# Conditioning panels accumulated on DVE, another order of the first chunks, and a tile-by-tile pass from the last layer norm to the first RMS norm

## The reference

```python
s_c = silu(c); s_cc = silu(c_ctx)
for i in range(DEPTH):                                   # DEPTH = 2
    m  = (s_c  @ ada_w[i] + ada_b[i]).reshape(B, 9, 1, D)
    mc = (s_cc @ ada_w[i] + ada_b[i]).reshape(9, D)      # the context's
    x = half_step_ffn(x, m[:, 0], m[:, 1], m[:, 2], ...)
    ...
# half_step_ffn: y = (silu(a) * u) @ w_out with a, u = split(modulate(x) @ w_in)
#                x = layer_norm(DN_ALPHA * x + 0.5 * gate * y, g, b)
```

## Time and profile before

| | us |
|---|---|
| median of 3 runs | 3017.51 |
| lowest and highest | 3009.21 and 3021.42 |
| profiled execution | 3014.72 |
| its span | 3012.9 |
| TensorE busy (96% of the span) | 2898.0 |
| DVE busy (59%) | 1765.8 |
| ACT busy (45%) | 1356.7 |

### The profile page before, as it was taken

How to read it: one execution, slowest core, us unless ns; L and a number is a source line. 1 busy time by engine, 2 the same in 40 slices (tenths; PEclk the granted TensorE clock), 3 DMA queues, 4 the chain that set the end, 5 groups by cost and what they waited for, 6 DMA issues and landing times. The chain is left out here.

```text
span 3012.9 us, 51229 instructions
## 1 busy us (share of the span) xinstructions
PE 2898.0 (96%) x19396; PEld 2540.7 (84%) x19396; DVE 1765.8 (59%) x2644; ACT 1356.7 (45%) x1928; POOL 375.3 (12%) x306
## 2 busy tenths in 40 slices
PE   6999999899999999999899999999999999999998
PEld 3667765677888889888899989899999998988998
DVE  2323224267766667666545866757855577566784
ACT  1222213125655544554344544455644454436563
POOL 2111100113110110211100120201101002020110
PEclk8999999999999999999999999999999999999999
DMA  9986354751565655465435505245555451533564
GB/s 325 285 252 195 103 164 130 198 168 49 158 184 154 194 183 160 148 195 182 142 120 167 161 28 176 92 134 153 170 162 161 137 154 57 160 114 112 161 179 135
DMA packets 586157, 474.79 MB, mean 158 GB/s; under 512 B 28721, under 2 KB 547889, under 8 KB 585665
## 3 DMA queue, kind: packets, MB, share of 16 engines
q1 hardware_dynamic: 584464, 460.44, 49.8%
q0 software_dynamic: 1520, 11.95, 1.3%
HBM read 471.23 MB, written 4.72 MB: 158 GB/s over the span
## 5 line engine op out<-in xcount | busy, mean ns | idle before, releaser
L2309 DVE TENSOR_TENSOR low<-raw,high 128x1024 fp32r<-128x1024 f32 (+1 forms) x744 | 904.6, 1219 | 801.0 <-ACT high L2079 798.6
L2079 ACT CAST high<-raw 128x1024 fp32r<-128x1024 f32 (+1 forms) x744 | 768.1, 1034 | 987.9 <-PE PS L1987 604.7
L1985 PE MATMUL PS<-NHh,high 128*128 128x272 f32 (+1 forms) x2304 | 669.0, 290 | 11.4 <-DVE NHl L1752 6.9
L1987 PE MATMUL PS<-NHh,low 128*128 128x272 f32 (+1 forms) x2304 | 660.8, 287 | 0.0
L1986 PE MATMUL PS<-NHl,high 128*128 128x272 f32 (+1 forms) x2304 | 660.0, 286 | 0.0
L1985 PEld LDWEIGHTS PS<-NHh,high 128*128 128x128 f32 x2304 | 433.3, 188 | 16.9 <-issue 9.1
L1986 PEld LDWEIGHTS PS<-NHl,high 128*128 128x128 f32 x2304 | 433.9, 188 | 0.8
L1987 PEld LDWEIGHTS PS<-NHh,low 128*128 128x128 f32 x2304 | 433.6, 188 | 0.0
L1983 PE MATMUL PS<-XX,high 128*128 128x512 f32 x966 | 347.8, 399 | 0.0
L1985 PE MATMUL PS<-XX,high 128*128 128x512 f32 (+1 forms) x752 | 273.5, 364 | 6.9 <-DVE XX L2370 4.4
L1982 PE MATMUL PS<-XX,low 128*128 128x256 f32 x966 | 272.4, 282 | 1.4 <-DVE XX L2370 1.0
(11 more groups left out here) (351 smaller groups left out, 4868.7 us busy)
## 6 DMA issues: line engine op xcount, KB each, us to landing
raw<-w_in_dram SPq DMA_DIRECT2D x416, 256.0 KB, 3.0
raw<-ffn_w_in_dram SPq DMA_DIRECT2D x352, 256.0 KB, 3.4
part<-ada_w_dram SPq DMA_DIRECT2D x184, 256.0 KB, 4.2
raw<-w_ffn_in_dram SPq DMA_DIRECT2D x176, 256.0 KB, 3.2
raw<-ffn_w_out_dram SPq DMA_DIRECT2D x160, 256.0 KB, 3.1
raw<-w_branch_dram SPq DMA_DIRECT2D x96, 256.0 KB, 3.0
raw<-w_ffn_out_dram SPq DMA_DIRECT2D x80, 256.0 KB, 3.0
part_sg<-ada_w_dram SPq DMA_DIRECT2D x48, 256.0 KB, 3.0
```

Of the source, the lines that this page charges most:

```text
L1985: nc.tensor.matmul(out, wh, xh, start=begin, stop=False)
L1987: last = nc.tensor.matmul(out, wl, xh, start=False, stop=end)
L2079: nc.scalar.copy(high[:, slot, 0:nk, :], raw[:, slot, 0:nk, :]).then_inc(s_high, 1)
L2309: nc.vector.tensor_tensor(low[:, slot, 0:nk, :], raw[:, slot, 0:nk, :], high[:, slot, 0:nk, :].bitcast(F32), ALU.subtract).then_inc(s_low, 1)
```

## The change

Three edits are made together.

1. **Conditioning.** Parts of panels 4 to 35 are no longer multiplied on TensorE. `ada_accumulate` on DVE multiplies a row tile of the part by the column `silu` and adds it to an accumulator of 128x512: two operations for a part, and four for the first six panels (`ADA_BOTH` = 10), whose context half is needed too. It is called in `split_low(S)` for the parts hosted at S-4. TensorE sums four accumulators over the partitions with a column of ones (`ada_sum`, two chunks behind the turn's last host). Hosts, buffers and dues are new; SP's `load_part` now waits for `s_adak`, which DVE raises.
2. **Start.** The first chunks of units 0 and 1 come first, with panel 3's parts between them, then the second chunks of both; the low tiles of X are made two at a time; `keep_warm` issues idle matmuls; chunk 1's weights are loaded before panel 1.
3. **Norms.** DVE scales each tile by `xg` and rdev, ACT squares it with the bias `xb`, and DVE writes `H` beside that. The second constants have a semaphore of their own.

```diff
-ADA_HOSTS = ((0, 32, 80), (44, 24, 24), (68, 16, 24))
+ADA_HOSTS = ((2, 12, 16), (14, 10, 16), (24, 10, 16), (34, 6, 8), (45, 38, 72))
+ADA_BOTH = 10
@@ def turn_host(t)
-    return HOST[4 * TURN * t - 1]
+    return min(HOST[4 * TURN * t - 1] + 2, 83)
@@ buffers
+        ROWS, TAIL, TOP = range(4, 11), 11, (12, 13)
+        part_slot = [A % 4 if HOST[A] < 32 else A % 2 if HOST[A] < 44 else
+                     ROWS[A % 7] if HOST[A] < 68 else 11 + A % 3 for A in range(ADA_PARTS)]
+        def place(s, u, c):
+            return 2 * c + u if s is steps[0] and isinstance(u, int) and u < 2 else s["S0"] + len(s["kch"]) * u + c
@@ issue
-            due = HOST[before] + 4 if before is not None else {PSG: 47, PRS: 47, TAIL: 71}.get(part_slot[A], 1)
+            due = HOST[before] + 4 if before is not None else 3 + part_slot[A] if HOST[A] < 44 else 48 if HOST[A] < 68 else 71
@@ def load_part(A)
                 if before is not None:
-                    sp.wait_ge(s_ada, 4 * ADA_FIRST + before + 1)
+                    sp.wait_ge(s_adak, before + 1)
+                elif slot in ROWS:
+                    sp.wait_ge(s_chunk, steps[1]["S0"] + 4)
+                elif slot in TOP:
+                    sp.wait_ge(s_res, KT + 4)
@@ TensorE
+            def ada_sum(t):
+                pe.wait_ge(s_adak, 4 * TURN * t)
+                pe.wait_ge(s_adarow, max(1, t - 1))
+                for c in range(2):
+                    for x in range(TURN):
+                        both = TURN * t + x < ADA_BOTH
+                        if both or not c:
+                            last = nc.tensor.matmul(PS[32 * x:32 * x + 32, ROW_BANK + t % 2, :],
+                                                    ONEW[:, 2 * (TURN - x) - 1 - c:2 * (TURN - x) + 31 - c], ada_acc(t, x, c),
+                                                    start=not c, stop=bool(c) or not both)
+                last.then_inc(s_adasum, 1)
...
-                        for A in ada_parts(S + c):
-                            ada_part(ADA_FIRST + A // 4, A % 4)
+                        if isinstance(at, int) and at in sum_after:
+                            ada_sum(sum_after[at])
...
+                    if s is steps[0]:
+                        for c in range(2):
+                            for u in range(2):
+                                gemm_unit(u, u, 0, 0, c)
+                                if c == 0 and u == 0:
+                                    for q in range(4):
+                                        ada_part(3, q)
@@ DVE, def split_low(S, slot, nk)
+                for A in ada_parts(S - NSLOT if isinstance(S, int) else S):
+                    ada_accumulate(A)
+
+            def ada_accumulate(A):
+                n, c = ADA_FIRST + A // 4, A % 4
+                t, x = divmod(n, TURN)
+                slot = part_slot[A]
+                dve.wait_ge(s_part[slot], 32 * part_slot[:A + 1].count(slot))
+                if x == 0 and c == 0 and t > 1:
+                    dve.wait_ge(s_adasum, t - 1)
+                for y in range(2):
+                    k = 2 * c + y
+                    src = flat(parts_at[slot][:, 2 * y:2 * y + 2, :])
+                    for e in range(2 if n < ADA_BOTH else 1):
+                        acc, factor = ada_acc(t, x, e), silu[:, KT * e + k:KT * e + k + 1]
+                        if k == 0:
+                            ins = nc.vector.tensor_scalar(acc, src, factor, None, ALU.mult)
+                        else:
+                            ins = nc.vector.scalar_tensor_tensor(acc, src, factor, acc, ALU.mult, ALU.add)
+                        if y == 0 or e < (n < ADA_BOTH):
+                            link(ins)
+                ins.then_inc(s_adak, 1)
+                dve.wait_ge(s_adak, A + 1)
@@ ACT, last layer norm
-                        act.wait_ge(s_res, 6 * KT + KT)
-                        act.wait_ge(s_meta, 32)
-                        for v in range(4):
-                            rms_act_pair(act, 0, v, None)
+                        act.wait_ge(s_meta, 16)
+                        nc.scalar.activation(TQ[:, :, 0:N_META], H[:, :, 0:N_META], ACT.Square)
+                        for k in range(KT):
+                            act.wait_ge(s_modd, KT * 6 + k + 1)
+                            ins = nc.scalar.activation(TQ[:, k, N_META:T2], TC[:, k, 0:T], ACT.Square,
+                                                       bias=sm("xb")[:, k:k + 1])
+                            if k % 2:
+                                ins.then_inc(s_rsq, 1)
+                        act.wait_ge(s_con2, 16)
@@ DVE, last layer norm
-                        standardise(0)
-                        standardise(1).then_inc(s_modd, 1)
+                        for k in range(KT):
+                            nc.vector.scalar_tensor_tensor(TC[:, k, 0:T], TC[:, k, 0:T], sm("xg")[:, k:k + 1],
+                                                           RS[:, 1, 0:T], ALU.mult, ALU.mult).then_inc(s_modd, 1)
+                        for k in range(KT):
+                            dve.wait_ge(s_modd, KT * 6 + k + 1)
+                            nc.vector.tensor_scalar(H[:, k, N_META:T2], TC[:, k, 0:T], sm("xb")[:, k:k + 1], None,
+                                                    ALU.add).then_inc(s_res, 1)
```

More of the change, by code:

```diff
@@ L317, in two_block_kernel @@
         SC0 = 2 * (TURN - 1)
-        SCW = E1.take("SCW", [P, KT, SC0 + 32])
         adarow = E1.take("adarow", [P, T1])[:]
+        acc2 = E1.take("acc2", [P, PW])
+        scw_at = E1.at
+        acc3 = E1.take("acc3", [P, PW])
+        SCW = Region(scw_at).take("SCW", [P, KT, SC0 + 32])
+        ONEW = E1.take("ONEW", [P, 2 * TURN + 31])
+        silu = E1.take("silu", [P, 2 * KT])
         e1_end = E1.at
@@ L494, in behind, with finished @@
                     two(i)
+        def place(s, u, c):
+            return 2 * c + u if s is steps[0] and isinstance(u, int) and u < 2 else s["S0"] + len(s["kch"]) * u + c
+        def finished(s, u):
+            return s["S0"] + len(s["kch"]) * (u + 1) + 4 + (s is steps[0] and isinstance(u, int) and u == 0)
         def unit_of(S):
@@ L514, in issued_after @@
             return [A for A in range(ADA_PARTS) if issue[A] == S] if isinstance(S, int) else ()
+        sum_after = {turn_host(t): t for t in range(1, ADA // TURN)}
         turn_unit = [None] + [unit_of(turn_host(t)) for t in range(1, ADA // TURN)]
@@ L1716, in rms_squares @@
         def rms_squares(m):
-            return SQ if m and m % 2 == 0 else TN
+            return TN if m % 2 else SQ if m else TQ
         def rms_pe_pair(pe, m, v):
@@ L1800, in load_unit @@
                         sp.wait_ge(s_low, S + 1)
-                    if not isinstance(S, int) or S:
+                    if isinstance(S, int) and S < NSLOT:
+                        if S > 1:
+                            load(raw[:, S], s_raw[S], s["src"](S - 2, *SHALLOW[1]))
+                    else:
                         load(raw[:, slot], s_raw[slot], s["src"](u, k0, nk))
@@ L1807, in _ @@
                 if n == 1:
-                    load(raw[:, 0], s_raw[0], steps[0]["src"](0, *SHALLOW[0]))
+                    for u in range(2):
+                        load(raw[:, u], s_raw[u], steps[0]["src"](u, *SHALLOW[0]))
                 for c in range(4):
@@ L1873, in ada_fold, with keep_warm @@
                 return last
+            def keep_warm(n):
+                for _ in range(n):
+                    nc.tensor.matmul(PS[0:32, 4, :], SCW[:, 0, 0:32],
+                                     raw0[:, 4 * FIRST_PLACE[0], 0:2, :].rearrange("p a n -> p (a n)"),
+                                     start=True, stop=True)
             pe.wait_ge(s_sc4, 3)
-            for n in (0, 2, 1, 3):
+            for n in (0, 2, 1):
+                if n == 2:
+                    keep_warm(9)
                 if n == 1:
@@ L1950, in rows_ready, with gemm_unit @@
                         pe.wait_ge(s_hl, s["hid0"] + 2 * c)
-                def gemm_unit(u, p, S, slot0):
+                def gemm_unit(u, p, S, slot0, only=None):
                     kch = s["kch"]
                     for c, (k0, nk) in enumerate(kch):
-                        pe.wait_ge(s_low, S + c + 5)
+                        if only is not None and c != only:
+                            continue
+                        at = S + c if only is None else place(s, u, c)
+                        pe.wait_ge(s_low, at + 5)
                         rows_ready(u, c, k0 + nk)
@@ L1960, in gemm_unit @@
                                 pe.wait_ge(s_oln, half_first(s["layer"], 2) + 1)
-                        slot = (slot0 + c) % NSLOT
+                        slot = (slot0 + c) % NSLOT if only is None else at
                         for j in range(2):
-                            if isinstance(S, int) and S + c == 0 and j == 1:
+                            if isinstance(at, int) and at == 1 and j == 1:
                                 ada_columns(0)
@@ L2099, in residual_rows @@
```

(10 more changed lines are left out.)

79 lines of the change are left out of this document (41 added, 38 removed).

## The result

| | before | after |
|---|---|---|
| median | 3018.39 us | 3333.64 us |
| lowest and highest | 3009.21 and 3021.42 | 3330.33 and 3335.39 |
| profiled execution's span | 3012.9 | 3333.6 |

The changed kernel is slower by 10.5%: the ratio is 1.105, with a 95% interval of 1.1026 to 1.1074. The prediction was 3290 us, from 3215 to 3350, so the sign and the range held, and the forecast was 44 us short.

What follows compares the result with a forecast made beforehand. TensorE, 96% busy, bounds the kernel before; after the change SP's in-order load queue, tied to DVE's accumulations, does. 3014.7 us + 283 (later milestones up to q) - 8 (norm) = 3290 us, range 3215 to 3350.

Steps and rivals of the forecast that it cites:

- The bound and the sign: SP's load queue, waiting for DVE's accumulations, lets one chunk be in flight at a time; slower, chance 0.93.
- TensorE was to idle for `low`: First third of the changed profile: TensorE idles before L2035, released by `low`, and its busy share falls to some 85%.
- The untied rival: SP's load queue: the tie doesn't bind because parts or raws run further ahead; 2902 us, chance 0.05.
- The cycle: From one accumulated chunk to the next: 8.2 us plus the accumulation, 9.7 to 14.0 us, where TensorE needs 5.5.
- The operation: One DVE accumulation on 128x512: 0.72 us, bounds 0.63 and 0.80; 219 us in all.
- longer-cycle rival: Load cycles: 6.7 us landing in 47 two-part cycles, 38 more, DVE's epilogues exposed, 24 more; 3350 us, chance 0.12.
- The 8 us for the bias tables: Values and keys, chunks 73 to 86: bias tables arriving by DMA there add 8 us.
- Chunks 42 and 43 end near 477 us, now near 348: End of the glu: these chunks finish 129 us later than in the kernel before.
- The start: First chunks: the new order begins near 34 us instead of 38.8 and wins 4 us.
- The norm: Last layer norm to first RMS norm: tile-by-tile work on DVE, ACT and TensorE saves 8 us, bounds 6 and 9.
- The first rival: TensorE's clock stays low between chunks, adding some 35 to 40 us; 3327 us, chance 0.12.
- What TensorE gives up: Conditioning: 128 parts, 100.3 us, and 10.9 us of waits leave TensorE, 10 us of sums come; alone 101 us gained.

Runs made afterwards that it cites:

- one wait more: Kernel before, TensorE still multiplying the parts; a part reloading a buffer behind raw chunk S in SP's list also waits for `low` of chunk S: 3193.86 us.
- one chunk of slack: Changed kernel with each part's buffer reload one chunk further down SP's list, no work changed: 2981.65 us.
- the hosts moved: Changed kernel, reloads two chunks later, hosts of the last 72 parts moved (53 onto the `res` step), raw chunk 72 ahead of parts waiting for the residual tile: 2936.64 us.
- two chunks of slack: Changed kernel with each part's buffer reload two chunks further down SP's list, no work changed: 2950.69 us.
- the thinned run: Changed kernel, accumulations after each panel's first cut to 8 of 512 columns: 2923.23 us with two chunks of slack, 3232.08 us with SP's list as it was.

## Why the prediction was right, and where it was short

**The bound and the sign: right.** TensorE gave up the parts and the kernel became slower, since the time was set by the load queue. This was read from the order of SP's list and DVE's, not from busy times, and the runs with one wait more and with one chunk of slack show it from both sides. TensorE 87% busy (some 85 was said), the DMA share of 0.34 to 0.47 by stretch, and SP's waits of 5.7 us each (5 was said, in 68 places; it is 112, since two parts of a chunk wait each for itself) are as the prediction asked for. One sign was not: TensorE was to idle for `low`, and its longest waits from 60 to 960 us on that line end with DVE's eviction, which stands behind the accumulations in DVE's list:

```profile
PE PS L2035 <- DVE SG L2671: 91.5, 9, 13.0
...
PE PS L2035 <- DVE low L2368: 43.8, 12, 6.0
```

This comes on top within a cycle and doesn't lengthen the ring, in which TensorE has no part: the waits end while the next raw is still on its way. The untied rival (2902), with "it decides as soon as the accumulation awaited stands before the `low` of a chunk already landed", names what the repair does; it gave 2950.7 and, with the hosts moved, 2936.6.

**The cycle: right in its mechanism, short in size.** The prediction's milestones, as differences between one and the next, K(S) being the end of the accumulation behind `low` of chunk S:

| | predicted | measured | short by |
|---|---|---|---|
| to K(6) | 71 | 72.4 | 1.4 |
| K(6) to K(41) | 387 | 412.2 | 25.2 |
| K(41) to K(49) | 38 | 44.5 | 6.5 |
| K(49) to K(68) | 205 | 210.5 | 5.5 |
| K(68) to the norm | 21 | 21.4 | 0.4 |
| norm to K(72) | 42 | 41.1 | -0.9 |
| K(72) to K(86) | 152 | 158.7 | 6.7 |
| K(86) to q's rope | 10.7 | 6.9 | -3.8 |
| sum | 926.7 | 967.7 | 41 |

The forecast was 44 us under the median, and by the profiled executions' spans, which this table goes by, 46. Of these, 41 are in the table; 2 are chunks that q was to find ready and didn't; the norm gave 1 more than said; and 4 lie behind the first RMS norm (last paragraph of this section). Four terms were mis-sized, 44 us together (the other rows give 3 back):

- *The operation.* Taken as 0.72 us; the rows above show 0.75 and starts 0.787 apart, while the first of each panel takes 0.48. Leaving out what POOL adds, the accumulations of the ring sum to 201 us where 196 was said: 5 us.
- *POOL beside DVE.* Not in the sum at all, 18 us, all of it in K(6) to K(41); the section on the hardware has it.
- *The rest of the cycle, the second part above all.* "I take 8.2 plus the accumulation, since a first part of two is issued while DVE still works on the second": right for the part's issue, but its transfer lies ahead of the raw. From the end of an accumulation to the end of the next `low` the changed kernel takes 8.1 us with one part, and with two 8.5 in the glu, 8.2 in `res` and 8.9 among values and keys. Over all three stretches that is 14 us. The prediction had 6.7 us of landing for two parts in its longer-cycle rival, 38 us, and gave it 0.12. The cycles lie between the forecast and that rival (3350), nearer to the forecast's in `res` (11.25 against 11.1) and to the rival's among values and keys (12.00 against 11.9). The rival's other 24 us, for epilogues of DVE in the cycle, didn't come: the 8.1 us with one part leave nothing for them.
- *The end of the glu.* K(41) to K(49), 6.5 us short. Chunk 42's `low` ends 9.4 us behind K(41), not 8.2; TensorE then waits 3.0 us for DVE's eviction, which stands behind the accumulation of that chunk; and the low clock takes 2.4.

The 8 us for the bias tables are in the 10.7 of the last row, while their DMAs fly at 804 to 865 us, so the last two rows belong together: 165.6 us where 162.7 was said. In the three cycles with these DMAs the raw takes 6.3, 7.3 and 6.0 us from issue to `high`, in the stage's other cycles with two parts 5.1 to 5.9: some 3 us together. So 5 of the 8 us covered by luck what the cycles are short there.

**One misreading.** "Chunks 42 and 43 end near 477 us, now near 348": the matmul at 347.76 in the earlier trace rows works on `GG`, the operand of the `res` step, so it ends chunk 44. The glu ended at 342.54, and at 510.44 in the changed kernel, where 477 was said. The sum didn't rest on it, since it ran through the norm and the rope, which were read rightly.

**The start: wrong.** 4 us were forecast and none showed. "The third chunk then ends near 59 us" took 7 us for a chunk that was to follow the wait; it took 8.0 in the changed kernel and 8.2 in the start alone, half of it at the lower clock, and the parts that TensorE had done in the old order's wait weren't set against the gain. The milestone K(6) came 1.4 us late.

**The norm: right.** 8 us with bounds of 6 and 9; 9.0 in the trace of all edits together, 10 (6 to 14) alone.

**The first rival (3327 us): fell within the glu, and its nearness to 3334 is chance.** The granted clock did fall (0.67 to 0.82 by stretch, against 0.98 to 1.00 before), but within the glu the wait is longer than what the clock takes, and lifting it brought no chunk sooner. At the end of the glu it cost 2.4 us. The rule of the Trainium skill that was weighed (TensorE: Matmul & The Clock Gate, section HAM oscillation) tells of a kernel that starts each tile at the low clock behind its wait; the trace agrees with it at chunk 42.

**What TensorE gives up: 101 us forecast.** With the start and the norm the untied kernel was to be 113 us under before; the version with two chunks of slack is 68 under. Of the 45 missing, 27 are DVE's load (the thinned run), 4 the start, and 14 came back with the hosts moved. These aren't strictly additive, but they leave little. TensorE's busy time fell by 82.6 us in the best version, where 100.3 less 10 was said.

Some 4 us lie between the first RMS norm and the end (317.0 later at the one, 320.7 at the other). That stretch, in which no run changes anything, takes 1545.0 to 1555.1 us in the traces of all twelve kernels, so they are within its scatter.

## What to carry to other kernels

When work moves to another engine, look first at who waits for it: a queue that is served in order (here SP's) turns a harmless wait for old work into a ring if the new owner does that work behind something that the queue itself has still to deliver. Such a ring shows in no busy share, only in the order lists and in the queue's waits, and its price is its length: load, conversion and accumulation one behind the other, once per item. Here the cure added no work, only one or two positions in the list; and when the ring is gone, look again at what the new owner's load costs, since it was hidden until then.

## What the runs showed of the hardware

An accumulation of DVE takes 0.75 us, but 1.78 where it starts while POOL multiplies two tiles (starts and durations in the changed kernel, POOL, then DVE):

```profile
82.79 1.81 POOL L2798 TENSOR_TENSOR GG<-SG,GG 128x512 fp32r<-128x512 f32 x1 [17.08 <-ACT GG L2257]
```

```profile
82.23 1.23 DVE L2368 TENSOR_TENSOR low<-raw,high 128x1024 fp32r<-128x1024 f32 x1 [8.35 <-ACT high L2136]
83.37 1.78 DVE L2389 SCALAR_TENSOR_TENSOR RS<-part,silu,RS 128x512 f32<-128x512 f32 x1
85.19 0.75 DVE L2389 SCALAR_TENSOR_TENSOR acc_both<-part,silu,acc_both 128x512 f32<-128x512 f32 x1
```

There are 19 places where POOL's L2798 overlaps an accumulation, and in all 19 one operation takes 1.0 us longer; the TENSOR_SCALAR of 128x512 goes from 0.49 to 1.51. Without the overlap none does. The long operation ends 0.55 us behind POOL's (85.15 against 84.60), less than its own 0.75, as if it had begun only near POOL's end. Of the 19 places 18 lie in the ring and cost it 18 us. The thinned run shows the same beside an operation of 8 columns, which takes 0.23 us alone (POOL, then DVE):

```profile
123.65 1.82 POOL L2798 TENSOR_TENSOR GG<-SG,GG 128x512 fp32r<-128x512 f32 x1 [20.33 <-ACT GG L2257]
```

```profile
124.23 1.26 DVE L2389 SCALAR_TENSOR_TENSOR RS<-part,silu,RS 128x8 f32<-128x8 f32 x1
```

Its 12 accumulations beside L2798 take 1.22 to 1.26 us, so the 1.0 us is the same for an operation with a sixty-fourth of the data: it is a wait until POOL is done, not a slower pace. The Trainium skill, SBUF — State Buffer, section Who interferes with whom, says that GpSimd and DVE share a port pair as an exclusive lock, which matters for a DVE instruction with two inputs in SBUF beside a GpSimd instruction that reads SBUF, and for a `tensor_scalar` in a two-port mode; the trace agrees with the wait. A run without POOL's work wasn't tried, so that the ports are its cause is argued from the overlaps.
